# FFN1 in two phases: gate and up columns first, with 32 of 44 pairs as seven block products, the activation stored to DRAM, and the down projection afterwards with its sums kept in PSUM over up to four groups

## The reference

```python
def swiglu(h, w_in, w_out):
    g, u = jnp.split(h @ w_in, 2, axis=-1)
    return (jax.nn.silu(g) * u) @ w_out
...
        m_lat = (jax.nn.silu(c) @ ada_w[l] + ada_b[l]).reshape(b, N_MOD, 1, d)
        m_ctx = (jax.nn.silu(c_ctx)[None, :] @ ada_w[l] + ada_b[l]).reshape(1, N_MOD, 1, d)

        x = x + 0.5 * m_lat[:, 2] * swiglu(modulate(rms_norm(x, norm1_g[l]), m_lat[:, 0], m_lat[:, 1]),
                                           ffn1_w_in[l], ffn1_w_out[l])
        ctx = ctx + 0.5 * m_ctx[:, 2] * swiglu(modulate(rms_norm(ctx, norm1_g[l]), m_ctx[:, 0], m_ctx[:, 1]),
                                               ffn1_w_in[l], ffn1_w_out[l])
```

## Time and profile before

| | before |
|---|---|
| median of three runs | 2781.34 us (2780.56 to 2782.48) |
| the profiled execution | 2780.76 us |
| its span in the profile | 2779.0 us |
| TensorE / VectorE / ScalarE busy | 2707.2 / 1954.6 / 1033.8 us |
| clock granted to TensorE, mean | 0.992 |

### The profile page before, as it was taken

One profiled execution on the slowest core, in us unless ns is written; L12 is line 12 of the kernel. 1 busy time (PEld: TensorE's weight loads), 2 busy tenths in 40 slices (PEclk: granted clock), 3 DMA queues, 4 the chain that ended last, 5 costly groups with the idle time before them and its releaser, 6 DMA issues.

```text
span 2779.0 us, 33277 instructions
## 1 busy us (share of the span) xinstructions
PE 2707.2 (97%) x12667; PEld 2259.6 (81%) x12667; DVE 1954.6 (70%) x2116; ACT 1033.8 (37%) x1051; POOL 7.0 (0%) x15
## 2 busy tenths in 40 slices
PE   6999999999999999999999899999999999999998
PEld 4778888888888888888888788888987888888887
DVE  6856767675767667676767753487677788888866
ACT  6632212122121212221247532465454555554443
POOL 0000000000000000000000000000000000000000
PEclk9999999999999999999999999999999999999999
DMA  9956645555555557676766342342446555556563
GB/s 313 300 189 204 184 140 173 152 165 166 157 169 151 167 156 250 195 261 194 256 186 215 99 122 91 109 141 85 131 142 212 182 196 183 195 188 209 177 226 121
DMA packets 408021, 496.87 MB, mean 179 GB/s; under 512 B 19090, under 2 KB 277512, under 8 KB 407176
## 3 DMA queue, kind: packets, MB, share of 16 engines
q1 hardware_dynamic: 407196, 493.10, 56.1%
q0 software_dynamic: 496, 2.63, 0.3%
q10 hardware_dynamic: 252, 0.10, 0.0%
HBM read 493.69 MB, written 2.10 MB: 178 GB/s over the span
## 4 chain that ended last, share of the span: by engine, by line
PE 76%; DVE 9%; issue 5%; ACT 3%; DMA 1%; DVEq 0%; ACTq 0%; SPq 0%
PE py L1190 7%; PE py L1192 7%; PE py L1191 7%; PE pg L1190 5%; PE pu L1192 5%; PE pg L1191 5%; PE pu L1191 5%; PE pu L1190 5%; PE pg L1192 5%; DVE sraw L2327 2%; PE two L1604 2%; DVE wl L2316 2%; PE two L1606 2%; PE two L1605 2%; DVE wl L1767 1%
## 5 line engine op out<-in xcount | busy, mean ns | idle before, releaser
L1767 DVE TENSOR_TENSOR wl<-raw,wh 128x2048 fp32r<-128x2048 f32 x218 | 499.5, 2291 | 452.8 <-ACT wh L704 452.6
L704 ACT ACTIVATE wh<-raw 128x2048 fp32r<-128x2048 f32 x218 | 416.6, 1913 | 867.6 <-PE py L1192 469.9
L1190 PE MATMUL py<-ah,wh 128*128 128x512 f32 x704 | 274.9, 390 | 6.1 <-DVE xy L1949 2.4
L1191 PE MATMUL py<-al,wh 128*128 128x512 f32 x704 | 274.3, 390 | 0.0
L1192 PE MATMUL py<-ah,wl 128*128 128x512 f32 x704 | 274.2, 390 | 0.0
L1190 PE MATMUL pu<-hh,wh 128*128 128x512 f32 x656 | 255.5, 390 | 0.0
L1190 PE MATMUL pg<-hh,wh 128*128 128x512 f32 x656 | 255.5, 390 | 0.0
L1191 PE MATMUL pg<-hl,wh 128*128 128x512 f32 x656 | 255.5, 390 | 0.0
L1191 PE MATMUL pu<-hl,wh 128*128 128x512 f32 x656 | 255.5, 389 | 0.0
L1192 PE MATMUL pg<-hh,wl 128*128 128x512 f32 x656 | 255.5, 389 | 0.0
L1192 PE MATMUL pu<-hh,wl 128*128 128x512 f32 x656 | 255.5, 389 | 0.0
(11 more groups left out here) (447 smaller groups left out, 5427.3 us busy)
## 6 DMA issues: line engine op xcount, KB each, us to landing
raw<-in_ffn_w_in SPq DMA_DIRECT2D x130, 1024.0 KB, 5.1
chunk<-in_ada_w SPq DMA_DIRECT2D x189, 512.0 KB, 3.9
raw<-in_ffn_w_out SPq DMA_DIRECT2D x84, 1024.0 KB, 5.1
sraw<-in_ffn_w_in SPq DMA_DIRECT2D x40, 1024.0 KB, 5.1
raw<-in_ada_w SPq DMA_DIRECT2D x64, 512.0 KB
raw<-in_mix_w_in SPq DMA_DIRECT2D x30, 1024.0 KB
accc<-in_ada_w SPq DMA_DIRECT2D x35, 512.0 KB, 4.8
raw<-in_mix_w_out SPq DMA_DIRECT2D x16, 1024.0 KB
```

The source lines that it names most:

```text
L704: nc.scalar.activation(wh[:, slot % 2, :], raw[:, slot, :], ACT.Copy).then_inc(wh_ready, 1)
L1190: mm(out_ap, w[0], xh_ap, start=first, stop=False, skip_group_check=True)
L1191: mm(out_ap, w[0], xl_ap, start=False, stop=False, skip_group_check=True)
L1767: tt(wl[:, slot % 2, :], raw[:, slot, :], wh[:, slot % 2, :].bitcast(F32), ALU.subtract).then_inc(wl_ready, 1)
```

## The change

Phase A forms the activation of all 44 pairs, phase B the whole down projection.

- Pairs 3 to 11 stay two slabs of 48 matmuls each, written out (steps STD0 to PROD0 - 1). Meanwhile VectorE forms sums and differences of blocks of x (`form`, `form_lo`, and `last_form` during the first pair behind them).
- Pairs 12 to 43 are seven block products each (P1, P5, P6, P3, P7, P2, P4), each of 8 k-tiles by 3 matmuls of 256 columns, 24 matmuls. The blocks are the two halves of k by gate and up, and latent and context tokens. VectorE adds weight blocks in place (`w_sum`, four of 128 x 1024 for a pair); both splits work on half slots of 128 x 1024 (seven each for a pair) in a ring of four; ScalarE copies three partial results out of PSUM and applies the silu in two pieces, VectorE combines them (`up_ctx`, `up_lat`, `gate_lat`, `pair_gate`).
- GpSimd stores each pair's activation (128 x 512) to DRAM; phase B loads it again, 1 MB for a group of four pairs, split like weights (`act_high`, `act_low`).
- Phase B has 44 steps of 48 matmuls of 512 columns: three parts (groups 0 to 3, 4 to 7, 8 to 10), in each the four quarters of the output, in each the groups of the part. The sum of a quarter stays in its banks over the part, so it leaves PSUM three times: in part 0 by ScalarE (`copy_out`), in part 1 by VectorE (`add_out`), in part 2 by VectorE with the gates.
- Chunks have two buffers throughout, and lie as three tables say: STD_CHUNKS for a standard slab, S_CHUNKS for a pair of products, B_CHUNKS for a step of phase B.
- The loops of FFN1 are written out.

```diff
+PAIRS = DFF // P
+STD_PAIRS = 9
+FIRST_S = EARLY + STD_PAIRS
+S_PAIRS = PAIRS - FIRST_S
+FORMS = ("P1", "P5", "P6", "P3", "P7", "P2", "P4")
+STD0 = ADA_SLABS
+PROD0 = STD0 + 2 * STD_PAIRS
+DOWN0 = PROD0 + len(FORMS) * S_PAIRS
+PARTS = ((0, 4), (4, 8), (8, GROUPS))
+STEPS = [(part, q, g) for part, (g0, g1) in enumerate(PARTS) for q in range(4) for g in range(g0, g1)]
+X_STEP = len(STEPS) - 12
+MIX0 = DOWN0 + len(STEPS)
+TURNS = MIX0 // 4 - PROD0 // 4
 
 S_CQ, S_RQ, S_CKV, S_KR, S_RK, S_RV, S_RG = 0, 4, 8, 10, 11, 15, 23
 S_UQ, S_UKV, S_OUTR, S_OUTM, MSLABS = 31, 34, 36, 44, 52
...
-    SINGLE_CHUNKS = 2 * KT
-    FIRST_AT = {s: tuple(range(4 * s - 24, 4 * s - 20)) for s in range(6, 10)}
-    SINGLE_AT = {s: tuple(range(4 * s, 4 * s + 4)) for s in range(4)}
-    SINGLE_AT.update({s: tuple(range(4 * s - 4, 4 * s)) for s in range(5, 9)})
-    CHUNK0 = KT * PAIRS0
-    FIRST_LOADS = chunk_slots(KT)
-    SINGLE_LOADS = chunk_slots(SINGLE_CHUNKS)
...
+    STD_CHUNKS = spans((5, 2, 5, 2, 5, 3, 4, 5) + 6 * (4,) + (5, 4, 0, 0), 0)
+    S_CHUNKS = spans(21 * (3,) + (1,) + (2, 2, 1, 2, 1, 2, 1, 2, 1, 2), 4 * KT)
+    B_CHUNKS = spans(2 * (4 * (2,) + 4 * (3, 3, 2)) + 12 * (0,), SINGLES + KT)
...
+            def chunk_load(c):
+                sp.wait_ge(chunk_free, max(c, 1))
+                t, r = c % KT, c // KT
+                col = 5 * D + r * CH if c < SINGLES else 2 * D + (r - SINGLES // KT) * CH
+                sp.dma_start(chunks[c % 2], ada_w[0, t * P:(t + 1) * P, col:col + CH]).then_inc(chunk_loaded[c % 2], 16)
+
+            def chunks_ahead(span):
+                for c in span:
+                    if c + 2 < SINGLES + DUALS:
+                        chunk_load(c + 2)
...
+            for k in range(PAIRS):
+                pool.wait_ge(act_ready, k + 1)
+                tile = (2, 0, 1)[k] if k < EARLY else k
+                pool.dma_start(scratch[tile], act_buf[k % 2][:]).then_inc(act_stored[k % 2], 16)
...
+            for s in range(2 * STD_PAIRS - 2):
+                if s % 2 == 0:
+                    std_silu(EARLY + s // 2)
+                static_split(STD0 + s + 2)
+                if s in (2, 4, 6):
+                    form_hi((s - 2) // 2)
+            std_silu(FIRST_S - 1)
...
+            for k in range(FIRST_S, PAIRS):
+                at_x, _, at_z = pair_banks(k)
+                form_high_half(k, 0)
+                form_high_half(k, 1)
+                form_high_half(k, 2)
+                if k > FIRST_S:
+                    pair_silu(k - 1)
+                form_high_half(k, 3)
+                pair_keep(k, 0, p1a[:], at_x, a_p1)
+                if k == FIRST_S:
+                    form_hi(3)
+                form_high_half(k, 4)
+                if k > FIRST_S:
+                    se.wait_ge(act_ready, k)
+                pair_keep(k, 1, tv[:, 1, :], at_z, a_p5)
+                form_high_half(k, 5)
+                pair_keep(k, 2, tv[:, 0, :], at_x, a_u2)
+                form_high_half(k, 6)
+
+            def act_high(g):
...
+            def down_high(j):
+                slot, turn = b_place("w", j)
+                se.wait_ge(b_loaded[slot], 16 * turn)
+                se.wait_ge(slab_used, (prod(PAIRS - 1, 4 + 2 * j) if j < 2 else DOWN0 + j - 2) + 1)
+                nc.scalar.activation(wh[:, j % 2, :], raw[:, slot, :], ACT.Copy).then_inc(wh_ready, 1)
...
+            def copy_out(j):
+                part, q, _ = STEPS[j]
+                for d in range(4):
+                    if d < 3:
+                        se.wait_ge(y_done, 12 * part + 3 * q + d + 1)
+                    else:
+                        se.wait_ge(slab_used, DOWN0 + j + 1)
+                    nc.scalar.activation(xy[:, :, 4 * q + d, :], pair(down_banks[d][:]), ACT.Copy).then_inc(y_free, 1)
...
+            for j in range(len(STEPS)):
+                s = j - X_STEP
+                if s == 11:
+                    squares(s)
+                if j + 2 < len(STEPS):
+                    if STEPS[j + 2][1] == 0:
+                        act_high(STEPS[j + 2][2])
+                    down_high(j + 2)
+                else:
+                    static_split(MIX0 + j + 2 - len(STEPS))
+                if step_last(j) and STEPS[j][0] == 0:
+                    copy_out(j)
+                if 8 <= s < 11:
+                    squares(s)
+                if 0 <= s < 8:
+                    spread(s)
             roots(0)
...
+            def pair_product(k, pos, bank_, first, last):
+                n = prod(k, pos)
+                pe.wait_ge(wl_ready, n + 1)
+                slot, o = half_slot(n)
+                name = FORMS[pos]
+                for t in range(HALF):
+                    if name in ("P1", "P2", "P4"):
+                        part, t0 = {"P1": (0, 0), "P2": (0, HALF), "P4": (1, HALF)}[name]
+                        xh_ap, xl_ap = hh[:, part, t0 + t, :], hl[:, part, t0 + t, :]
+                    elif name == "P7":
+                        xh_ap, xl_ap = hh[:, 1, t, :], hl[:, 1, t, :]
+                    else:
+                        f = ("P5", "P6", "P3").index(name)
+                        xh_ap, xl_ap = fhs[f][:, t, :], fls[f][:, t, :]
+                    w = (wh[:, slot, o + t * P:o + (t + 1) * P], wl[:, slot, o + t * P:o + (t + 1) * P])
+                    ins = three(bank_[:, 0:LAT], w, xh_ap, xl_ap, first and t == 0, t == HALF - 1)
+                ins.then_inc(slab_used, 1)
+
...
+            def form(k):
+                if k == 0:
+                    whole(flt[0], 1, 0)
+                    whole(fht[1], 0, 0)
+                    link(whole(fht[0], 1, HALF))
+                    tt(flt[0][:], flt[0][:], fht[0][:], ALU.subtract).then_inc(form_sum, 1)
+                    ve.wait_ge(form_sum, 1)
+                    link(tt(flt[1][:], flt[0][:], fht[1][:], ALU.subtract))
+                elif k == 1:
+                    nc.vector.memset(nm[:, 2:3], 0.0).then_inc(form_sum, 1)
+                    link(whole(fht[2], 0, HALF))
+                    tt(flt[2][:], flt[1][:], fht[2][:], ALU.add).then_inc(form_sum, 1)
+
...
+            def last_form():
+                a = slice(0, HALF)
+                tt(h21[0][:], hh[:, 0, a, :].bitcast(F32), hh[:, 1, a, :].bitcast(F32), ALU.subtract)
+                link(tt(h21[1][:], hl[:, 0, a, :].bitcast(F32), hl[:, 1, a, :].bitcast(F32), ALU.subtract))
+                tt(h21[1][:], h21[0][:], h21[1][:], ALU.add).then_inc(form_sum, 1)
...
+            for k in range(FIRST_S, PAIRS):
+                span = S_CHUNKS[k - FIRST_S]
+                half_low(k, 0)
+                if k > FIRST_S:
+                    up_ctx(k - 1)
+                w_sum(k, 0, 1, True)
+                half_low(k, 1)
+                if k == FIRST_S:
+                    std_mult(k - 1)
+                w_sum(k, 0, 2, True)
+                if k > FIRST_S:
+                    gate_lat(k - 1)
+                w_sum(k, 1, 2, False)
+                half_low(k, 2)
+                w_sum(k, 0, 3, True)
+                half_low(k, 3)
+                if k > FIRST_S:
+                    pair_gate(k - 1)
+                else:
+                    last_form()
+                    form_lo(3)
+                for n in range(3):
+                    for c_ in span[n:n + 1]:
+                        chunk_step(c_)
+                    half_low(k, 4 + n)
+                up_lat(k)
+
...
+            def add_out(j):
+                part, q, _ = STEPS[j]
+                for d in range(4):
+                    k = 4 * q + d
+                    if d < 3:
+                        ve.wait_ge(y_done, 12 * part + 3 * q + d + 1)
                     else:
...
+                    if part == 1:
+                        ve.wait_ge(y_free, Y_F1 + k + 1)
+                        ins = tt(xy[:, :, k, :], pair(down_banks[d][:]), xy[:, :, k, :], ALU.add)
+                    else:
+                        ve.wait_ge(x_folded, k + 1)
+                        for x_, gate, o in ((xl, g1l, 0), (xc, g1c, LAT)):
+                            ins = stt(x_[:, k, :], down_banks[d][:, o:o + LAT], gate[:, k:k + 1], x_[:, k, :], ALU.mult, ALU.add)
+                    ins.then_inc(y_free, 1)
...
+                if 1 <= s <= 8:
+                    fold(s - 1)
+                if step_last(j) and STEPS[j][0]:
+                    add_out(j)
+                if s == 11:
+                    square_adds(s)
+                if j + 2 < len(STEPS):
+                    if STEPS[j + 2][1] == 0:
+                        act_low(STEPS[j + 2][2])
+                    down_low(j + 2)
+                else:
+                    static_split(MIX0 + j + 2 - len(STEPS))
+                if 8 <= s < 11:
+                    square_adds(s)
+                for c_ in B_CHUNKS[j]:
+                    chunk_step(c_)
+                if -1 <= s < 7:
+                    turn(s + 1)
             ve.wait_ge(ada_summed, 20)
             link(ts(g3l[:], ml[:, 8 * KT:9 * KT], 0.5, None, ALU.mult))
             roots(0, 0)
```

626 lines of the change are left out of this document (367 added, 259 removed).

## The result

The changed kernel takes 2895.22 us (median, 2893.49 to 2897.09) against 2781.32 for the kernel before: ratio 1.0412, 95% interval 1.0398 to 1.0425, 114 us slower.

What follows compares the result with a forecast made beforehand. TensorE was taken to bound FFN1, busy 1371.88 of 1377.94 us. Matmuls of 1319.6 plus 93 of stops made 1413, 35 more than 1377.9, so 2816 us against 2781.3; range 2766 to 2850.

Steps and rivals of the forecast that it cites:

- The matmuls: FFN1: seven products take 20.16 a pair against 21.76, gaining 51 us over 32 pairs; matmul sum 1319.6 against 1370.9.
- Rival D: Products: matmuls of 256 columns lie 0.130 apart instead of 0.120, no gain, 2867; given no chance apart from Rival C's.
- VectorE beside the products: Pairs of products: VectorE needs 20.0 to 21.1 a pair, TensorE 20.16 still bounds by a hair; takings cost 5 us.
- Rival C: Products: VectorE bounds them too, needing 21.1 a pair by durations; 2841, or 2869 with dearer 1024-wide operations; chance 0.17.
- Standard slabs: Standard stage: VectorE bounds, ending after 220.2 with reloads at 3.8, against 195.8 of matmuls; 24.4 us of waiting.
- The clock: TensorE behind stops: eight to ten long stops lose about 1.7 each to slower clock; 7 us taken.
- First pair: First pair of products: the last form's high part delays ScalarE's queue, P3 waits 9.8, then 3 more; 13 us.
- last pair: Last pair of products: two takings in a row, 9.4, with about 2 in hand on VectorE; 7.5 us.
- part 0's copies: Phase B, part 0: ScalarE's copies behind the high part stop TensorE 2.8 at four quarters' ends; 11.2 us.
- Part 1: Phase B, part 1: VectorE's additions at steps 23, 27 and 31 come 4.7, 8.5 and 2.8 late; 16 us.
- Rival B: Chunk waits absent, reloads usable 2.5 us after release instead of 3.8: faster, 2769, or 2762 without the clock term; chance 0.20.

Runs made afterwards that it cites:

- b_no_chunks: The changed kernel without chunk operations (but the first of each sixteen, the others a tiny memset) and without their reloads; takings of the sums stay: 2758.43 us.
- a_slab_late: The changed kernel with chunk reloads issued ahead of the weight slab instead of behind it, in the standard stage alone, two buffers as before: 2880.86 us.
- a_three: The changed kernel with a third buffer for the 128 single chunks; dual chunks keep two: 2845.26 us.
- a_no_reload: The changed kernel without loads of the chunks behind the first two; VectorE does every chunk operation on what the two buffers hold: 2783.39 us.
- b_mended: The changed kernel with third single-chunk buffer, standard-stage reloads ahead of slabs, part 0 copies ahead of the high half, last form's high part behind P5's copy: 2822.20 us.
- c_even17: The b_mended edits with 17 standard pairs instead of 9, chunks placed by each step's VectorE room, second taking of a dual round held back: 2805.66 us.
- d_even17c: c_even17 with new chunk tables: at most two dual chunks a step in part 1, 30 there instead of 35, two rounds of takings instead of three: 2773.76 us.
- d_even17c_two: d_even17c with two buffers for the single chunks instead of three, all else equal: 2838.20 us.

## Why the prediction was wrong

The direction was right, the size was not: 35 us slower were forecast, 114 came, above the range's end of 2850. In FFN1 1413 us were forecast and 1500.3 came; half of the 87 between them lie in the standard slabs. Step by step:

**The matmuls: right.** Pairs run at 20.16 wherever nothing stops them, and b_no_chunks, 22 us below the kernel before, shows that the gain is real. The rule of the Trainium skill ("TensorE: Matmul & The Clock Gate", Back-to-back issue gap), 109.2 ns a matmul of 256 columns, would be 18.3 a pair; it does not occur here. Rival D falls.

**VectorE beside the products: price right, its waits missing.** 1.22 for 1024 was exact. VectorE is busy 609.0 us over the 32 pairs, 19.0 each, about as priced (19.1 less 1.0 of waiting, and 0.9 of takings). But the middle pairs lost 24.8 where I had 5: waits for reloads beside the products were put at nothing, without a reason, and VectorE waited 35.3 us for chunks there. The median landing is 5.2 (3.8 before in the same stretch); that the 120 half slabs on the same queue are the reason is likely, but no run shows it. Without reloads the loss is 3.4. Rival C falls: this was no bound by work.

**Standard slabs: the failed step.** "I take 3.8, just under both." I had priced every reload alike and put some 44 us of waiting on VectorE (127, less 80 for the 64 operations, less the 3.5 hidden); 84.4 came. In this stage the 12 reloads issued within 2 us behind a weight slab (four of them behind two half slabs) landed 6.4 to 9.2 us after their issue, those issued 8 us or more behind one after 3.5 to 5.8. The 40 us of waiting that I had not priced are nearly the whole miss: the stage was to end after 220.2 and took 263.6. TensorE lost 67.8 for 24.4. The rows were not wrong, but they were read at a place where the reload is issued ahead of the slab; that the change moves the slab ahead of it stands in SyncE's queue, which I had not compared. That order alone is worth 17 us (a_slab_late), a third buffer 35 (a_three).

**The clock: the second failed step.** I had 7 us; 43 lie in slow matmuls. A row of TensorE's timeline:

```profile
243.72 0.79 PE L1378 MATMUL pu<-hh,wh 128*128 128x512 f32 x1 [6.27 <-DVE wl L1998]
```

And the window around it (0.52 is the granted clock):

```profile
243.00:249.00 6.00, 5.28 (x13) 4.17 (x14) 5.97 (x5) 2.63 (x2) 0.00 (x0) 0.52 0.83 261
```

Behind a gap of 6.3 us matmuls lie 0.43 to 0.59 apart instead of 0.227, at the lower level, 1.2 GHz, and that slab takes 13.35. The price of a long stop, 1.7 us, was about right on the average (43 over 24 stops, 1.8); I had the number of stops wrong, "eight to ten" where 24 of 2.4 us or more came, the norm's not counted. One alone can differ: behind the three equal stops of 2.64 us in part 0 the granted clock was 1.00 once and 0.66 twice, and the slab behind them lost 0.1, 1.7 and 1.7.

```profile
1178.00:1183.00 5.00, 4.89 (x22) 4.09 (x23) 4.90 (x4) 1.43 (x3) 0.00 (x0) 1.00 0.38 115
1224.50:1229.50 5.00, 4.98 (x15) 3.97 (x16) 4.76 (x15) 1.33 (x3) 0.00 (x0) 0.66 0.18 71
1272.50:1277.50 5.00, 4.94 (x15) 3.92 (x16) 3.13 (x3) 1.38 (x3) 0.00 (x0) 0.66 0.25 102
```

Not all of the 43 were lost. 17.6 of them lie in the standard slabs, where VectorE sets the end of the stage and, after its first split, waited only for chunks; slower matmuls there came out of TensorE's gaps. The 26 outside them stand against my 7.

**First pair, last pair, part 0's copies: right in the main.** 13.6 for 13, 9.6 for 7.5, and stops of 2.80 as priced, but three of them and not four: at the fourth quarter's end the low split was later than the copy (4.8). Without reloads, in a_no_reload, all four are 2.80. The first pair by its rows, ScalarE, then TensorE:

```profile
455.29 1.91 ACT L926 ACTIVATE hh<-h21l 128x2048 fp32r<-128x2048 f32 x1 [9.08 <-DVE h21l L2213]
457.10 1.04 ACT L951 ACTIVATE wh<-raw 128x1024 fp32r<-128x1024 f32 x1
458.05 0.36 ACT L958 ACTIVATE tv<-py 128x256 f32<-128x256 f32 x1
...
458.46 0.58 PE L1378 MATMUL py<-fhs,wh 128*128 128x256 f32 x1 [8.96 <-ACT tv L958]
```

The form's high part, a half slot and the copy stand in the queue as foretold, and P3 waits 8.96 for the 9.8 priced. The stop of 3 that was to follow at P7 did not come; slow matmuls behind the long stop made up for it, so that 13.6 lies so near to 13 is in part luck. The last pair is one stop of 6.7 and slow matmuls behind it. That the form's place in ScalarE's queue cost anything is not shown: moving it (b_mended) left the first pair as long, because P7 then waits 8.56. Part 0's other 9.2 are that fourth stop and slow matmuls.

**Part 1: right mechanism, half the size.** 33.2 for 16. The additions at the ends of steps 23, 27 and 31 stop TensorE for 5.8, 9.3 and 7.9 us where 4.7, 8.5 and 2.8 were priced; a stop of 3.2 in step 17 for a low split was not foreseen, nor were 5.5 us of slow matmuls. The longest stop, VectorE, then TensorE:

```profile
1474.31 1.28 DVE L2136 SCALAR_TENSOR_TENSOR accl<-chunk,cs,accl 128x1024 f32<-128x1024 f32 x1 [3.08 <-DMA chunk<-in_ada_w]
1475.51 1.28 DVE L2136 SCALAR_TENSOR_TENSOR accc<-chunk,cs,accc 128x1024 f32<-128x1024 f32 x1
1476.70 2.48 DVE L2322 TENSOR_TENSOR xy<-py,xy 128x512 f32<-128x512 f32 x4
...
1477.54 0.77 PE L1378 MATMUL py<-ah,wh 128*128 128x512 f32 x1 [9.28 <-DVE xy L2322]
```

The addition stands behind the chunks of the step before, as said, and 3.08 of the lateness is again a reload.

**Rival B** had its condition the wrong way round: reloads came later than 3.8, not sooner. Its kernel without waits for reloads was priced at 2762 to 2769; a_no_reload took 2783.4, and the waits were worth 112 us and not 47.

What stays open: how the 42.3 us of c_even17's part 1 divide between the third dual chunks, the takings that stand ahead of an addition and the five chunks more. d_even17c changed all three together. By the rows of the longest stop the two takings weigh most (8.9 us, against 2.5 for a dual chunk and 4.1 of waiting for its reload).

## What to carry to other kernels

When a change takes a buffer away from a ring, price the reload at each place by what stands ahead of it in the DMA queue, not by the median landing, and compare the issuing queue's order as well as the engines'. Add up the work of the second-busiest engine for each stretch and not over the whole, and spread what can be moved so that no stretch is over what it has, and so that nothing long stands just ahead of an operation that TensorE waits for. Here that, a third buffer, the other small edits and 24 pairs of products instead of 32 turned 4.1% slower into 0.25% faster. And a stop of TensorE can cost more than itself: some 1.8 us of slow matmuls came with each of the 24 longer stops. This is lost only where TensorE sets the pace; where another engine does, slower matmuls fit into the gaps. So count the stops, not only their sum.

## What the runs showed of the hardware

- A 512 KB reload issued 0.7 us behind a 1 MB slab was used 7.4 us after its buffer came free, the same reload issued ahead of the slab after 3.9. The 12 reloads of the changed kernel's standard stage that were issued within 2 us behind a slab or two half slabs landed after 6.4 to 9.2 us.
- The DMA engines carried 267 GB/s at a share of 0.83 over 372 us (d_even17c) with TensorE busy 370.8 of 372.5, so the traffic as such was not the limit; d_even17c_two differs in the number of buffers alone and lost 67 us more there.
- Matmuls of 256 columns held 0.120 us from start to start over nine pairs in a row, 1,512 matmuls in 181.44 us, as in the earlier trace rows.
- Behind three equal stops of 2.64 us the granted clock was 1.00 once and 0.66 twice in the next 5 us: the length of a stop alone did not decide it.
